# Moving w_ada steps, an attention order and a rotation in a two-layer hybrid transformer kernel

## The reference

```
h = layer_norm(x) * (1 + sc1) + sh1
x = layer_norm(ALPHA * x + g1 * mixer(h), ln1_g, ln1_b)
h = layer_norm(x) * (1 + sc2) + sh2
x = layer_norm(ALPHA * x + g2 * moe(h), ln2_g, ln2_b)
```

## Time and profile before

| | us |
|---|---|
| median of 3 runs | 1836.05 (1834.81 to 1836.21) |
| the profiled execution | 1837.3 |
| its span | 1835.5 |
| TensorE busy | 1718.6 (94%) |
| VectorE busy | 1169.5 (64%) |
| ScalarE busy | 939.7 (51%) |
| GpSimd busy | 222.2 (12%) |
| DMA | 393.28 MB, mean 214 GB/s |

### The profile page before, as it was taken

How to read it: one execution, slowest core, us unless ns; L and a number is a source line. 1 busy time by engine, 2 the same in 40 slices (tenths; PEclk the granted TensorE clock), 3 DMA queues, 4 the chain that set the end, 5 groups by cost and what they waited for, 6 DMA issues and landing times.

```text
span 1835.5 us, 27531 instructions
## 1 busy us (share of the span) xinstructions
PE 1718.6 (94%) x11564; PEld 1514.1 (82%) x11564; DVE 1169.5 (64%) x1288; ACT 939.7 (51%) x1057; POOL 222.2 (12%) x233
## 2 busy tenths in 40 slices
PE   5998997999899899799989999999999999989999
PEld 2886875888688688588769889899999998979998
DVE  2546558899963756889887565555446656555443
ACT  4434435877543453587756354354445545345442
POOL 0420011000034001000004500200001610110000
PEclk9998997999999999899999999999999999999999
DMA  9883566899858334499956445456655544545552
GB/s 364 305 270 123 198 212 251 337 375 373 290 169 274 132 111 172 162 380 389 334 200 206 127 138 161 138 185 206 208 186 192 173 127 138 184 138 185 187 189 83
DMA packets 207305, 393.28 MB, mean 214 GB/s; under 512 B 6128, under 2 KB 143344, under 8 KB 191312
## 3 DMA queue, kind: packets, MB, share of 16 engines
q1 hardware_dynamic: 204768, 381.71, 60.0%
q0 software_dynamic: 1712, 7.50, 1.1%
q10 hardware_dynamic: 704, 2.33, 0.3%
HBM read 390.46 MB, written 1.05 MB: 213 GB/s over the span
## 4 chain that ended last, share of the span: by engine, by line
PE 73%; DVE 10%; ACT 5%; issue 5%; POOL 4%; DMA 2%; SPq 0%; POOLq 0%; DVEq 0%; ACTq 0%
PE ps L546 21%; PE ps L547 20%; PE ps L548 20%; DVE low L1900 4%; ACT whi L1326 2%; PE ps L644 2%; POOL TB L2780 1%; DVE small L1962 1%; PE ps L847 1%; DMA AR<-in_w_ada 1%; PE ps L830 1%; DMA raw<-in_w_gu 1%; PE ps L663 1%; PE ps L815 1%; DVE T L2321 1%
## 5 line engine op out<-in xcount | busy, mean ns | idle before, releaser
L1900 DVE TENSOR_TENSOR low<-raw,whi 128x2048 fp32r<-128x2048 f32 x310 | 712.6, 2308 | 400.4 <-ACT whi L1326 398.9
L1326 ACT ACTIVATE whi<-raw 128x2048 fp32r<-128x2048 f32 x310 | 591.0, 1912 | 330.1 <-PE ps L548 302.4
L546 PE MATMUL ps<-Hh,whi 128*128 128x256 f32 x1536 | 441.1, 287 | 14.9 <-DVE Bl L2342 14.9
L547 PE MATMUL ps<-Hl,whi 128*128 128x256 f32 x1536 | 436.4, 284 | 0.0
L548 PE MATMUL ps<-Hh,low 128*128 128x256 f32 x1536 | 436.2, 284 | 0.0
L546 PE MATMUL ps<-whi,Hh 128*128 128x256 f32 (+1 forms) x896 | 294.8, 329 | 32.0 <-DVE low L1900 13.6
L546 PEld LDWEIGHTS ps<-Hh,whi 128*128 128x128 f32 x1536 | 296.4, 193 | 32.5 <-issue 16.1
L547 PEld LDWEIGHTS ps<-Hl,whi 128*128 128x128 f32 x1536 | 296.6, 193 | 0.5
L548 PEld LDWEIGHTS ps<-Hh,low 128*128 128x128 f32 x1536 | 296.5, 193 | 0.0
L547 PE MATMUL ps<-low,Hh 128*128 128x256 f32 (+1 forms) x896 | 290.1, 324 | 0.0
L548 PE MATMUL ps<-whi,Hl 128*128 128x256 f32 (+1 forms) x896 | 289.5, 323 | 0.0
(11 more groups left out here) (325 smaller groups left out, 2155.6 us busy)
## 6 DMA issues: line engine op xcount, KB each, us to landing
raw<-in_w_gu SPq DMA_DIRECT2D x80, 1024.0 KB, 5.4
raw<-in_w_ff SPq DMA_DIRECT2D x66, 1024.0 KB, 5.1
raw<-in_w_in SPq DMA_DIRECT2D x58, 1024.0 KB, 6.0
raw<-in_w_d SPq DMA_DIRECT2D x40, 1024.0 KB, 5.8
raw<-in_w_gate SPq DMA_DIRECT2D x32, 1024.0 KB, 5.5
ada<-in_w_ada SPq DMA_DIRECT2D x18, 1024.0 KB, 7.2
G<-in_w_ada SPq DMA_DIRECT2D x16, 1024.0 KB, 8.3
raw<-in_w_out SPq DMA_DIRECT2D x16, 1024.0 KB, 5.1
```

What stands on the lines that cost most here:

```text
L546: pe.matmul(out, lhs[0], rhs[0], start=start, stop=False)
L547: pe.matmul(out, lhs[0], rhs[1], start=False, stop=False)
L1326: act.activation(wide(i, whi), wide(i, raw), ACT.Copy).then_inc(*up("w_hi", i))
L1900: dve.tensor_tensor(wide(i, low), wide(i, raw), wide(i, whi).bitcast(F32), ALU.subtract).then_inc(*up("w_lo", i))
```

## The change

The steps' tables put steps 31 to 33 at a new place `x1` (after the first tile's transposes in the router), 34 and 35 at `rt`, and 36 to 41 after the last `put_back` of layer 0, where 32 to 34 stood; layer 1 keeps 42 to 47. Steps 32, 33 and 35 are loaded into `Bf0` and `Bf1`, which lie on the buffers Bh and Bl of the branch inputs. The sums move too, and ScalarE's copies with them. In the attention of the first block (both layers) ScalarE's `values_hi(0)` comes ahead of `next_gate(1)`, and VectorE's `values_lo(0)` ahead of scored(2), with `next_gate(1)` behind `values_lo(1)`. `rotate` handles both token tiles in one go.

```diff
@@ the tables
-MOD_TAKEN = [{"qa": (8, 9)} | {place: (10 + i,) for i, place in enumerate(MOD_PLACES[1:])},
-             {"qa": (35,)} | {place: (36 + i,) for i, place in enumerate(MOD_PLACES[1:13])}]
-MOD_SUMMED = [{"vd2": 4, "pa": 13, "xT": 14, "moe": 15} | {f"qk{i}": 5 + i // 2 for i in (1, 3, 5)} | {f"at{i}": 8 + i // 2 for i in (1, 3, 5, 7, 9)},
-              {"vd1": 16, "vd2": 17} | {f"qk{i}": 18 + i // 2 for i in (1, 3, 5)} | {f"at{i}": 21 + i // 2 for i in (1, 3, 5)}]
+MOD_TAKEN = [{"qa": (8, 9)} | {place: (10 + i,) for i, place in enumerate(MOD_PLACES[1:22])}
+             | {"x1": (31, 32, 33), "rt": (34, 35), "ff": (36, 37, 38, 39, 40, 41)},
+             {"vd2": (42,), "qk1": (43,), "qk2": (44,), "qk4": (45,), "at0": (46,), "at1": (47,)}]
+MOD_SUMMED = [{"vd2": (4,), "pa": (13,), "xT": (14,), "rt": (15,), "moe": (16, 17), "ff": (18,)}
+              | {f"qk{i}": (5 + i // 2,) for i in (1, 3, 5)} | {f"at{i}": (8 + i // 2,) for i in (1, 3, 5, 7, 9)},
+              {"vd1": (19,), "vd2": (20,), "qk2": (21,), "qk5": (22,), "at2": (23,)}]
@@ the buffers
+        Bf = [nc.alloc_sbuf_tensor_at(f"Bf{i}", [P, 2048], F32, offset=start + 8192 * i) for i in range(2)]
-        mod_slot += [ada, G0, G1, ada, G0, G1, ada, G0, ada, G0, ada] + [AR0, ada] * 4 + [ada]
-        mod_slot += [ada, AR0, AR1, ada, AR0, ada, G0, G1, ada, G0, ada, G0, ada, G0, ada, G0]
+        mod_slot += [ada, G0, G1, ada, G0, G1, ada, G0, ada, G0, ada] + [AR0, ada] * 3 + [AR0, AR1, ada, Bf[0], Bf[1], ada, Bf[0]]
+        mod_slot += [ada, AR0, AR1, AR[:, 4096:6144], ada, AR0, ada, G0, ada, G0, ada, G0]
@@ SP
-            for s in (29, 30):
+            load_mod(sp, 29)
+            sp.wait_ge(*at("mm", "pv", 0, 2, 2))
+            load_mod(sp, 30)
+            load_mod(sp, 31)
+            load(number["A", 0, "pa", 1] + 7)
+            sp.wait_ge(*at("mm", "pa", 0, 3))
+            load_mod(sp, 32)
+            load_mod(sp, 33)
+            load(number["A", 0, "out", 3] + 7)
+            for s in (34, 35, 36):
                 load_mod(sp, s)
-            load(number["A", 0, "out", 3] + 7)
-            for s in (31, 32):
-                load_mod(sp, s)
             sp.wait_ge(*at("mm", "gather", 0, 3))
-            for s in (33, 34):
+            for s in (37, 38):
                 load_mod(sp, s)
             load(number["A", 1, "qa", 0] + 6)
-            for s in (35, 36):
+            sp.wait_ge(*at("y_lo", 0, 0, 1))
+            sp.wait_ge(*at("y_lo", 0, 1, 1))
+            for s in (39, 40, 41, 42):
                 load_mod(sp, s)
...
@@ TensorE: moe, after the transposes of the first tile; ffn; to_T
+                    if t == 0:
+                        mod_turn(l, "x1")
-                    for s in (32, 33, 34):
+                    for s in MOD_TAKEN[0]["ff"]:
                         mod_step(s)
+                    mod_sums(18)
-                to_T("rq", ("p_rot", "rq", l, 1), ("T_a", "rq", l))
+                to_T("rq", ("p_rot", "rq", l), ("T_a", "rq", l))
...
@@ ScalarE: moe; between the layers; attention
                 mod_turn(l, "xT")
+                mod_turn(l, "x1")
                 taken("A", l, "out", 3)
...
+                mod_turn(l, "rt")
...
+                    for j in (18, 19):
+                        mod_out(j)
                     ln(sid, 0)
-                    mod_out(16)
+                    mod_out(20)
...
                 turned(1, 0)
+                values_hi(0)
                 next_gate(1)
-                values_hi(0)
                 values_hi(1)
@@ VectorE: attention
                 turned(1, 0)
+                values_lo(0)
+                scored(2)
+                values_lo(1)
                 next_gate(1)
-                scored(2)
-                values_lo(0)
-                values_lo(1)
                 gate(2)
@@ GpSimd
-                    for t in range(2):
-                        c, s = (con(a)[:, 32 * t:32 * t + 32].unsqueeze(1).broadcast_to([P, 4, 32]) for a in ("cos2", "sin2"))
-                        v = halves(tile[name])[:, t, :].rearrange("p (h two i) -> p h two i", two=2, i=32)
-                        t4 = [T1[:, 1024 + 128 * i:1152 + 128 * i].rearrange("p (h i) -> p h i", h=4) for i in range(4)]
-                        rotate(v[:, :, 0, :], v[:, :, 1, :], c, s, t4, name, l, t)
+                    c, s = (halves(con(a)).unsqueeze(2).broadcast_to([P, 2, 4, 32]) for a in ("cos2", "sin2"))
+                    v = tile[name].rearrange("p (t h two i) -> p t h two i", t=2, two=2, i=32)
+                    t4 = [T1[:, 1024 + 256 * i:1280 + 256 * i].rearrange("p (t h i) -> p t h i", t=2, h=4) for i in range(4)]
+                    rotate(v[:, :, :, 0, :], v[:, :, :, 1, :], c, s, t4, name, l)
```

More of the change, by code:

```diff
@@ L240, in build @@
         H = sb("Hh", [P, 8, S], F32R), sb("Hl", [P, 8, S], F32R)
+        start = (nc.sbuf_base + 31) // 32 * 32
         B = sb("Bh", [P, 8, S], F32R), sb("Bl", [P, 8, S], F32R)
+        Bf = [nc.alloc_sbuf_tensor_at(f"Bf{i}", [P, 2048], F32, offset=start + 8192 * i) for i in range(2)]
         x, T1, T2 = sb("xs", [P, 2, D]), sb("T1", [P, 2048]), sb("T2", [P, 2048])
@@ L387, in mod_acc, with mod_acc_after @@
         def mod_acc(j):
-            return AR[:, 8448:8960] if j in (1, 3) else AR[:, 7936:8448]
+            return AR[:, 8448:8960] if j in (1, 3, 16, 18, 20) else AR[:, 7936:8448]
+        def mod_acc_after(j):
+            return [i for i in range(j) if (i in (1, 3, 16, 18, 20)) == (j in (1, 3, 16, 18, 20))][-1:]
         def mod_half(s):
@@ L491, in program_sp @@
             load(number["A", 0, "pb"] + 7)
-            for s in (29, 30):
-                load_mod(sp, s)
+            load_mod(sp, 29)
[6 more added lines that the diff above has]
+            load_mod(sp, 33)
             load(number["A", 0, "out", 3] + 7)
-            for s in (31, 32):
+            for s in (34, 35, 36):
                 load_mod(sp, s)
             sp.wait_ge(*at("mm", "gather", 0, 3))
-            for s in (33, 34):
+            for s in (37, 38):
                 load_mod(sp, s)
             load(number["A", 1, "qa", 0] + 6)
-            for s in (35, 36):
+            sp.wait_ge(*at("y_lo", 0, 0, 1))
+            sp.wait_ge(*at("y_lo", 0, 1, 1))
+            for s in (39, 40, 41, 42):
                 load_mod(sp, s)
-            for name, s in ((("ka",), 37), (("vd", 0), 38), (("vd", 1), 39), *((("qk", i), 40 + i) for i in range(6)),
-                            (("gate", GATE_ORDER[0]), 46), (("gate", GATE_ORDER[1]), 47)):
+            sp.wait_ge(*at("x_new", 0, "ff", 1))
+            load_mod(sp, 43)
+            for name, s in ((("qk", 0), 44), (("qk", 1), 45), (("qk", 3), 46), (("qk", 4), 47)):
                 load(number["A", 1, *name] + 7)
[L507 to L510, removed]
                 load_mod(sp, s)
@@ L650, in mod_turn @@
             def mod_turn(l, place):
-                if place in MOD_SUMMED[l]:
-                    mod_sums(MOD_SUMMED[l][place])
+                for j in MOD_SUMMED[l].get(place, ()):
+                    mod_sums(j)
                 for s in MOD_TAKEN[l].get(place, ()):
@@ L1182, in second_block @@
                 rows_by_cols(("nk", l), ("B", l, "nk"), ("head_d", "nk", l))
-                to_T("rq", ("p_rot", "rq", l, 1), ("T_a", "rq", l))
+                to_T("rq", ("p_rot", "rq", l), ("T_a", "rq", l))
                 rows_by_cols(("nv", l), ("B", l, "nv"), ("pj_d", "nv", l))
-                to_T("rk", ("p_rot", "rk", l, 1), ("T_a", "rk", l))
+                to_T("rk", ("p_rot", "rk", l), ("T_a", "rk", l))
                 rows_by_cols(("mq", l), ("B", l, "mq"), ("head_d", "mq", l))
@@ L1406, in mod_out @@
                 act.wait_ge(*at("mm", "step", mod_last[j]))
-                if j >= 2:
-                    act.wait_ge(*at("mm", "mod", j - 1 if j > 4 else j - 2))
+                for i in mod_acc_after(j):
+                    act.wait_ge(*at("mm", "mod", i))
                 if j == 4:
@@ L1543, in moe @@
                     taken("A", l, "gu", n, 1)
-                    if n == 0:
-                        mod_turn(l, "rt")
                     if n == 1:
@@ L1615, in first_block @@
                         if i == 0:
-                            act.wait_ge(*at("mm", "step", 36 if l else 11))
+                            act.wait_ge(*at("mm", "step", 41 if l else 11))
                         leave_bank(AR[:, 512 * i:512 * i + 512], ("qk", l, i), "pj_a", "qk", l, i)
@@ L1919, in mod_turn @@
             def mod_turn(l, place):
-                if place in MOD_SUMMED[l]:
-                    mod_fin(MOD_SUMMED[l][place])
+                for j in MOD_SUMMED[l].get(place, ()):
+                    mod_fin(j)
             def ln_factors(sid, t):
@@ L2011, in residual_and_lift @@
                 lift(sid, scale, bias, 0, *ready)
+                mod_turn(0, "ff")
                 half(1, 1)
```

## The result

The changed kernel takes **1807.05 us** (median of 4 runs, 1803.47 to 1810.82) against 1835.43 before on the same chip: ratio 0.9849, 95% interval 0.9824 to 0.9873, 28.4 us by the medians; the forecast was 1803.5. It was timed twice more beside the experiments, 1805.54 and 1805.37 us against 1836.63 and 1836.45: ratios 0.9833 (0.9817 to 0.9848) and 0.9835 (0.9822 to 0.9849). Over all 14 runs of the changed kernel the median is 1805.6, and the two later pairs give 31.1 us each; I take the gain as 31 us where 32.5 was forecast. The profiled execution of after is the shortest of its four: 1803.47, span 1801.7, granted clock 0.977; that of before had 1837.3 and 0.968.

The account below looks back on a forecast made before the run. TensorE was taken as the bound almost everywhere, except at waits the change touches. Terms -19.4 - 9.1 - 8.8 + 1.5 + 3.3 = -32.5 us gave 1803.5 us, range 1797 to 1814.

Parts of the forecast that it names:

- part 1: First block's attention, both layers: earlier values_lo(0) frees the third gate unit's bank; wait and low clock go, 19.4 us off.
- part 2: Second block's rotation, both layers: six wide GpSimd operations replace twelve, shortening TensorE's wait of 3.81 us; 9.1 us off.
- part 3: Layer 1 loses seven steps and three sums, the expert stage gets one sum more; net 8.8 us off.
- part 4: Router: steps at x1 fill a hole, but ScalarE's mod_outs and extra work at rt cost 1.5 us.
- part 5: Seam between the layers: added steps, sum and later transfers delay the transposes; costs 3.3 us.
- Rival B: Attention: another wait takes the place of the bank's, half of part 1's gain lost, 1813 us; chance 0.12.
- four to five holds: Second block's rotation: six wide GpSimd operations, 4.5 us, plus these stretches while VectorE runs long splits, 12.7 to 14.8 us.
- Rival C: Second block: the rotation is held as often as before, about 1 us gained instead of 9, 1811; chance 0.13.
- Rival E: Moved steps: the seven are exposed where they now stand, so part 3 is 0, 1812 us; chance 0.05.
- F: Layer 0's expert stage turns DMA-bound, slower than before, 1840 us or more; chance 0.02.
- Rival A: Router: filled holes keep TensorE's clock up through the gather, 5.5 us more gained, 1798; chance 0.12.
- Rival D: Seam's transfers come later or the router pays its upper end, +5 us, 1808.5; chance 0.11.

Follow-up runs that it names:

- e1: Kernel before with only the attention's two reordered lists, on ScalarE and VectorE: 1816.07 us against 1836.63, ratio 0.9882.
- e5: Kernel before with one VectorE operation moved, values_lo(0) ahead of next_gate(1), ScalarE's order untouched: 1815.82 us, ratio 0.9897.
- e2: Kernel before with only the rotation changed, six GpSimd operations of 128x256 per tensor for twelve of 128x128: 1831.57 us, ratio 0.9965.
- e9: Kernel before with ScalarE's mod_turn rt moved behind the sigmoid, from behind a weight split of the first expert: 1831.84 us against 1836.45, ratio 0.9973.
- e4_all: The changed kernel as it is, timed and profiled again beside its parts: 1805.54 us.
- e6: Changed kernel with ScalarE's copies of rq's and rk's turned tiles ahead of the square of nk: 1804.60 us, ratio 0.9838.
- e3: Changed kernel with the attention's order and the rotation put back as before, leaving the moved steps: 1829.70 us, ratio 0.996.

## Why the prediction was right, and where it was not

| term | forecast | shown |
|---|---|---|
| part 1, order in the attention | -19.4 | -19.4 (e1, e5) |
| part 2, rotation | -9.1 | -6.3 (e2) |
| part 3, steps out of layer 1 | -8.8 | -8.5 |
| part 4, router up to place | +1.5 | +2.6 |
| ScalarE's mod_out, the bank of step 31 | not in the sum | -3.7 (e9) |
| part 5, seam | +3.3 | +4.4 |
| sum | -32.5 | -30.9 |

The measured gain is 31 us. The total came out near because two errors of opposite sign nearly met: 2.8 us too much for the rotation, 1.1 too little each for router and seam, against 3.7 that were not seen. Parts 1 and 3 came as reasoned; that the rest closed the sum this well is luck. The sum of the shown terms leaves out the gather's clock: in the profile of after the gather takes 4.07 us instead of 6.22, of which 0.7 go into a longer wait right behind it, so 1.5 us more in that profile, which e4_all doesn't have.

**Part 1.** Every step held: the bank counted in the code, TensorE ready 7.43 us earlier, 2.57 and 2.00 of low clock behind the waits. The 5 us to spare for divided(2) held too (VectorE is done with it at 171.97, TensorE's turned(2, 0) starts at 177.11); e5 shows that even a softmax 2.7 us later costs nothing. Rival B is out.

**Part 2.** GpSimd did what was forecast. Shifted by the 28.92 us by which its first operation starts earlier, rq is ready at 983.53 + 28.92 = 1012.45 (forecast 1012.2) and rk at 989.86 + 28.92 = 1018.78 (1019). The rule of the Trainium skill, SBUF — State Buffer, section "SBUF: two separate sides", that VectorE and GpSimd lock each other out, agrees with the five stretched operations as far as it goes; that all six of rq's would be met, the bound that the prediction took from it, didn't come about. The range for four to five holds, 12.7 to 14.8, should be 12.4 to 14.4 by the prediction's own hold of 11.9 / 6 us; nothing else hangs on that. The step that failed is the sum "2 x (3.81 - 0.2 - 0.6)": it takes the waits at the two transposes (0.2 and 0.6 forecast, 0.62 and none shown) for all that is left of the wait. It looked at the transposes of the two rotated tensors and not at what is late next. GpSimd's queue, from the end of rk's rotation, leads by its root, VectorE's nq and ScalarE's copy to ret_s(0), and its end moved by only 2.3 us a layer (22.79 us for both rotations before, 20.47 after; the holds are six in both kernels, 11.7 to 11.9 us together, so only the undisturbed time fell, from 24 x 0.46 to 12 x 0.73). To this comes what slack TensorE had there before: 0.3 us in layer 0, 1.5 in layer 1, where the low clock had held it longer. 2.6 + 3.8 = 6.4, and e2 shows 6.3; e6 shows that it was the copy. Rival C (held as often) had the mechanism right, over both tensors, and its price of 1 us wrong, since it charged the sixth hold to rq instead of rk; by the time it is out.

**Part 3.** From the seam's transposes to the end of layer 1's attention after gains 18.8 us; less 9.4 for part 1 that is 9.4, forecast 9.7; in e3, without the new order, the same stretch gives 8.0, so 7.1 to 8.5 net where 8.8 was forecast. The extra sum in the expert stage costs 0.9 (L1023 to L1052 in e3), as forecast. Rival E is out, and so is F: the expert stage of after is busy 30.00 of 30.00 us at 371 GB/s.

**Part 4.** ScalarE's two mod_outs cost x_turned(1) the 1.1 us forecast (the logits' product, L972, loses 1.0 against before), of which the higher clock gives 0.6 back. At rt the forecast let the hole of 1.08 take more than it did: the sum and both steps ran at the low clock, 1.85 + 1.93 + 1.94, and cost 2.2 us against the 0.4 allowed for. The term that was missing altogether is mod_turn's place on ScalarE. The prediction's list of ScalarE's additions was read for what it adds to the path; what an operation that leaves a place gives back there was not asked. Rival A foresaw a gain here, by another mechanism. Of the eight profiles with steps at x1 three have the gather at the full clock and five not or only in part; of the five without such steps none has it at full. That is a hint for it, and no more: it comes and goes in the same program. The Trainium skill, TensorE: Matmul & The Clock Gate, section "What's actually happening", lets recent activity set the clock, and says that at a kernel's start the number of matmuls at the low clock differs from run to run of the same kernel. The two times of one gather, 4.07 and 6.37 us, agree with the second, at a place inside the kernel. The first fits the low clock behind the wait of 7.43 us; but step 39 behind a wait of 2.04 us at the seam ran at the full clock (1.06 us) and step 41 behind one of 0.72 at half (1.93), so the wait just ahead doesn't tell the clock. Which execution gets the fast gather stays open.

**Part 5.** Step 41's transfer lands at 488.51, which in the time of before (16.16 us later) is 504.7; the estimate was 504. Behind it step and sum both took the upper end, 1.93 and 1.87: 4.4 in place of 3.3. The 0.3 for VectorE's two small operations didn't appear. Rival D's price was part 5's and part 4's upper end; it came half way.

One thing belongs to neither kernel: before's profile has a wait of 1.61 us for step 28's transfer, and the low clock behind it, 2.55 in all. No other profile has more than 0.21 us of it, not even e2, e3 and e9, which change nothing ahead of it. Of the 33.8 us between the two spans 2.6 are this, 0.9 the start, and some the low clock; that is why the spans differ by more than the medians.

## What to carry to other kernels

When a wait is taken away, follow every queue that the waiting or releasing engine feeds to its next meeting with the bound engine, and price the gain as the smaller of the two; a releaser named in the profile is only the last of several, so compare its end with the ends of all operations that give back a bank or buffer at that moment. For each operation that an edit moves ask both questions, what it delays where it goes and what it had held up where it was. And small extra work belongs into a wait for something else, not between two waits: the same steps and sum cost 4.4 us at the seam in one order and nothing in another.

## What the runs showed that was not expected

TensorE's granted clock differs between executions of the same program at the same places. The gather takes 4.07 or 6.37 us, and within the fully busy expert stage there are stretches of seven or eight products at 1.2 GHz, about 1.6 us lost each, with no wait ahead of them: in layer 0's stage none in two profiles of the changed kernel and one in the third (452 us, where the DMA share falls as well, from 0.96 to 0.26, and ScalarE's busy time from 3.30 to 0.63 of 4 us). The gather and this stretch make up 3.5 of the 4.8 us between the profiles of after and e4_all; the runs of one kernel spread by 3 to 9 us, and whether the rest of that is of the same kind isn't shown. Whether the pause of ScalarE and the DMAs is a cause or a result of it was not tried.
